# SSM groups of seven units with the gate inside, output halves under the last chunks, and a straight program

## The reference

```python
proj = u @ w_in
gl, cb, cc, cx, z, xbc, dt = jnp.split(proj, split_at, axis=-1)
...
xbc = jax.nn.silu(causal_depthwise_conv(xbc, ssm_conv_w) + ssm_conv_b.astype(xbc.dtype))
...
y = ssd_scan(xs * dt[..., None], dt * a, bs, cs)
y = y + d_skip.astype(jnp.float32)[:, None] * xs
y = y.reshape(bsz, seqlen, D_SSM) * jax.nn.silu(z.astype(jnp.float32))
yg = y.reshape(bsz, seqlen, SSM_GROUPS, D_SSM // SSM_GROUPS)
yg = yg * lax.rsqrt(jnp.mean(yg * yg, axis=-1, keepdims=True) + EPS)
y = (yg.reshape(bsz, seqlen, D_SSM) * ssm_norm_w.astype(jnp.float32)).astype(u.dtype)
p_ssm = y @ w_ssm_out
g_conv, g_ssm = jnp.split(jax.nn.sigmoid(gl), 2, axis=-1)
merged = g_conv * p_conv + g_ssm * p_ssm
```

## Time and profile before

| | us |
|---|---|
| median of 3 runs | 1856.3 |
| lowest and highest | 1855.08, 1859.28 |
| the profiled execution's own time | 1858.3 |
| its span in the trace | 1856.6 |
| TensorE busy | 1772.2 (95%) |
| VectorE, ScalarE, GpSimd busy | 1056.3, 794.6, 239.9 |

### The profile page before, as it was taken

How to read it: one execution, slowest core, us unless ns; L and a number is a source line. 1 busy time by engine, 2 the same in 40 slices (tenths; PEclk the granted TensorE clock), 3 DMA queues, 4 the chain that set the end, 5 groups by cost and what they waited for, 6 DMA issues and landing times.

```text
span 1856.6 us, 25724 instructions
## 1 busy us (share of the span) xinstructions
PE 1772.2 (95%) x8482; PEld 1456.2 (78%) x8482; DVE 1056.3 (57%) x1492; ACT 794.6 (43%) x1137; POOL 239.9 (13%) x312
## 2 busy tenths in 40 slices
PE   6889999999999999989999999999999989999997
PEld 4667777777888888868888888878897778888885
DVE  3677777775236666548855665685556343333333
ACT  4365666665222222355413443664433375224522
POOL 0101111110001220022111225211110200000001
PEclk8999999999999999989999999999999999999999
DMA  9143333332525664326655563111111323322331
GB/s 305 53 127 112 106 109 104 102 114 75 175 91 181 196 193 141 105 65 204 203 169 175 188 221 113 56 49 44 46 58 57 102 68 102 101 92 91 102 102 56
DMA packets 70501, 220.71 MB, mean 119 GB/s; under 512 B 8992, under 2 KB 17312, under 8 KB 70432
## 3 DMA queue, kind: packets, MB, share of 16 engines
q1 hardware_dynamic: 51664, 160.73, 26.8%
q0 software_dynamic: 17632, 56.83, 9.8%
q10 hardware_dynamic: 1136, 2.23, 0.4%
HBM read 217.52 MB, written 2.23 MB: 118 GB/s over the span
## 4 chain that ended last, share of the span: by engine, by line
PE 73%; DVE 10%; ACT 6%; DVEq 5%; issue 3%; ACTq 2%; DMA 1%; SPq 0%; POOL 0%
PE bank L385 19%; PE bank L386 19%; PE bank L387 19%; PE bank L1033 2%; PE bank L1034 2%; PE bank L1035 2%; DVE xs L717 1%; DVEq L738 1%; DVE bc L717 1%; PE bank L416 1%; DVE es L740 1%; PE bank L417 1%; PE bank L418 1%; PE bank L1086 1%; PE bank L1084 1%
## 5 line engine op out<-in xcount | busy, mean ns | idle before, releaser
L371 DVE TENSOR_TENSOR wlo<-wraw,whi 128x1024 fp32r<-128x1024 f32 x280 | 353.4, 1263 | 251.7 <-ACT whi L360 232.9
L360 ACT ACTIVATE whi<-wraw 128x1024 fp32r<-128x1024 f32 x280 | 295.8, 1058 | 441.2 <-PE bank L387 363.2
L385 PE MATMUL bank<-uhi,whi 128*128 128x512 f32 x1212 | 478.4, 395 | 2.1 <-DVE wlo L371 2.1
L386 PE MATMUL bank<-ulo,whi 128*128 128x512 f32 x1212 | 472.4, 390 | 0.0
L387 PE MATMUL bank<-uhi,wlo 128*128 128x512 f32 x1212 | 472.4, 390 | 0.0
L385 PE MATMUL bank<-vhi,whi 128*128 128x512 f32 x688 | 268.1, 390 | 0.0
L387 PE MATMUL bank<-vhi,wlo 128*128 128x512 f32 x688 | 267.7, 389 | 0.0
L386 PE MATMUL bank<-vlo,whi 128*128 128x512 f32 x688 | 267.6, 389 | 0.0
L385 PEld LDWEIGHTS bank<-uhi,whi 128*128 128x128 f32 x1212 | 228.1, 188 | 48.9 <-DVE wlo L371 2.6
L387 PEld LDWEIGHTS bank<-uhi,wlo 128*128 128x128 f32 x1212 | 228.0, 188 | 48.0
L386 PEld LDWEIGHTS bank<-ulo,whi 128*128 128x128 f32 x1212 | 228.3, 188 | 46.2 <-issue 0.2
(11 more groups left out here) (354 smaller groups left out, 2213.2 us busy)
## 6 DMA issues: line engine op xcount, KB each, us to landing
wraw<-in_units SPq DMA_DIRECT2D x280, 512.0 KB, 3.5
aring<-in_ada POOLq DMA_DIRECT2D x160, 256.0 KB, 3.7
slab<-in_ada SPq DMA_DIRECT2D x32, 256.0 KB, 6.9
es<-decay_rows POOLq DMA_DIRECT2D x32, 256.0 KB, 3.8
eac<-decay_rows POOLq DMA_DIRECT2D x32, 128.0 KB, 2.9
x<-in_xT SPq DMA_DIRECT2D x2, 1024.0 KB, 9.2
xr<-in_xT ACTq DMA_DIRECT2D x1, 2048.0 KB, 12.5
outT<-xr SPq DMA_DIRECT2D x8, 256.0 KB, 2.1
```

The lines of the kernel that those rows point to most:

```text
L360: act.activation(whi[:, at % SLOTS, :], wraw[:, at % RAW, :], ACT.Copy).then_inc(w_hi, 1)
L371: dve.tensor_tensor(wlo[:, at % SLOTS, :], wraw[:, at % RAW, :], whi[:, at % SLOTS, :].bitcast(f32), ALU.subtract).then_inc(w_split, 1)
L385: pe.matmul(out, wh, rhs_hi(k), start=first and k == 0, stop=False)
L386: pe.matmul(out, wh, rhs_lo(k), start=False, stop=False)
```

## The change

The order of the weight units and of the work around them is changed from the SSM groups to the output:

- Groups 1 to 7 have seven units: two of the six, one unit of the output's gate as unit 2, then the other four. ScalarE copies the gate's bank to `mg`. The taps stand in slots 0, 1, 3 and 4, the first z unit is unit 5, the second unit 6. ScalarE's silu of the first z unit and the squares are in slot 5; so is `pe_n`, behind a0; a1 is in slot 6. The silu of the second z unit comes ahead of the first convolution of the next group.
- `gate_ssm` is gone. A phase `tail` has the eighth unit of the gate, then the first halves of three outputs with b1 to b3 in between, then the second halves of these three in turn over the tiles, with `pe_n` after three tiles and waits for `f_fin` at each tile; then the fourth output's two halves. Four outputs are left for `ssm_out`.
- The sigmoids are eight activations on `mg`, one after the other, behind the last norm.
- Groups 1 to 7 and the output are straight code in place of loops; SyncE takes the units' order from a list.

```diff
 PHASES = [
     ("ssm0", 6, [0, 1, 2, 3, 0, 1], 1),
-    ("ssm", 12, [2, 3, 0, 1, 2, 3, 0, 1, 2, 3, 0, 1], 3),
-    ("ssm7", 6, [2, 3, 0, 1, 2, 3], 1),
-    ("gate_ssm", 8, [0, 1, 2, 3, 0, 1, 2, 3], 1),
-    ("ssm_out", 4, [0, 1], 4),
+] + [(f"ssm{g}", 7, [(7 * g - 1 + n) % 4 for n in range(7)], 1) for g in range(1, SSM_GROUPS)] + [
+    ("tail", 9, [3, 0, 1, 2, 3], 1),
+    ("ssm_out", 4, [0, 1], 2),
     ("conv", 4, [0, 1, 2, 3], 8),
     ("conv_out", 4, [0, 1, 2, 3], 2),
     ("w_o", 4, [0, 1, 2, 3], 2),
...
+
+
+def ssm_units():
+
+    gate, out = 6 * SSM_GROUPS, 6 * SSM_GROUPS + KT
+    order = list(range(6))
+    for g in range(1, SSM_GROUPS):
+        order += [6 * g, 6 * g + 1, gate + g - 1, 6 * g + 2, 6 * g + 3, 6 * g + 4, 6 * g + 5]
+    order += [gate + KT - 1] + [out + 2 * j for j in range(3)] + [out + 2 * j + 1 for j in range(3)]
+    return order + list(range(out + 6, out + 2 * KT))
...
-        def pe_slot(pe, k, g, par_, prev):
-
-            q = 1 - par_
-            if prev and k == 0:
-                pe_b(pe, g - 1, q, 0)
-                pe_a(pe, g - 1, q, 2)
-            if prev and k == 1:
-                pe_b(pe, g - 1, q, 1)
-                pe_a(pe, g - 1, q, 3)
-            if prev and k in (2, 3):
-                pe_b(pe, g - 1, q, k)
-            if prev and k == 5:
+        def pe_slot(pe, n, g, prev, here):
+            par_ = g % 2
+            if prev and n < 4:
+                pe_b(pe, g - 1, 1 - par_, n)
+                if n < 2:
+                    pe_a(pe, g - 1, 1 - par_, n + 2)
+            if here and n in (5, 6):
+                pe_a(pe, g, par_, n - 5)
+            if prev and n == 5:
                 pe_n(pe, g - 1)
-            if k in (4, 5) and not tail(g):
-                pe_a(pe, g, par_, k - 4)
-
-        def tail(g):
-            return isinstance(g, int) and g == SSM_GROUPS
...
-        def act_slot(act, k, g, par_, prev, it, ph, ku, here):
-
-            if 1 <= k <= 4 and here:
-                act_silu(act, g, par_, k - 1)
-            if here and k < 4:
-                act_conv(act, g, par_, k, it, ph, ku)
-            if prev and k == 0:
-                act.wait_ge(unit_done, 6 * g)
-                act_gate(act, 5, 1 if par_ else 3)
-            if here and k == 4:
-                wait_unit(act, ph, it, ku)
-                wait(act, S["f_y"], g)
-                act_gate(act, 4, PH[ph]["banks"][ku])
-            if k == 4 and prev:
+        def act_slot(act, n, g, prev, here):
+
+            par_, ph = g % 2, f"ssm{g}"
+            if prev and n == 0:
+                last = 7 * g - 2
+                act.wait_ge(unit_done, last + 1)
+                act_gate(act, 5, last % 4)
+            if here and n in (1, 2, 4, 5):
+                act_silu(act, g, par_, {1: 0, 2: 1, 4: 2, 5: 3}[n])
+            if here and n in (0, 1, 3, 4):
+                act_conv(act, g, par_, {0: 0, 1: 1, 3: 2, 4: 3}[n], 0, ph, n)
+            if here and n == 2:
+                wait_unit(act, ph, 0, n)
+                act.activation(mg[:, g - 1, :], bank(ph, n)[:], ACT.Copy)
+                act.drain().then_inc(freed(ph, n), 1)
+            if here and n == 5:
+                wait_unit(act, ph, 0, n)
+                act.wait_ge(S["f_y"], g)
+                act_gate(act, 4, PH[ph]["banks"][n])
+            if prev and n == 5:
                 act.wait_ge(S["f_y"], g)
                 act.activation(sqs[:], ys[:, 1 - par_, :, :], ACT.Square).then_inc(S["f_sq"], 1)
-            if k == 5:
+            if n == 6:
...
-        def dve_slot(dve, k, g, par_, prev, here):
-            if prev:
-                q = 1 - par_
-                if k == 0:
-                    dve_b(dve, g - 1, q, 0)
-                if k in (1, 2):
-                    dve_a(dve, g - 1, k + 1)
-                    dve_b(dve, g - 1, q, k)
-                if k == 4:
-                    dve_b(dve, g - 1, q, 3)
-                    dve.wait_ge(S["z_s"], 2 * g)
-                    dve.tensor_tensor(ys[:, q, :, :], ys[:, q, :, :], zs[:], ALU.mult).then_inc(S["f_y"], 1)
-            if here and k < 4:
-                dve_taps(dve, g, par_, k)
-            if k == 5:
...
+        def dve_slot(dve, n, g, prev, here):
+            par_ = g % 2
+            q = 1 - par_
+            if prev and n < 3:
+                if n > 0:
+                    dve_a(dve, g - 1, n + 1)
+                dve_b(dve, g - 1, q, n)
+            if prev and n == 4:
+                dve_b(dve, g - 1, q, 3)
+                dve.wait_ge(S["z_s"], 2 * g)
+                dve.tensor_tensor(ys[:, q, :, :], ys[:, q, :, :], zs[:], ALU.mult).then_inc(S["f_y"], 1)
+            if here and n in (0, 1, 3, 4):
+                dve_taps(dve, g, par_, {0: 0, 1: 1, 3: 2, 4: 3}[n])
+            if here and n == 5:
+                dve.wait_ge(S["cv_s"], 4 * g + 4)
+                for v in range(2):
+                    last = dve.tensor_scalar(ys[:, par_, v, :], xs[:, v, :], pcd("d_skip", 2 * g + v), None, ALU.mult)
+                last.then_inc(S["y_skip"], 1)
+                dve.drain()
+            if here and n == 6:
+                dve_a(dve, g, 0)
+                dve_a(dve, g, 1)
+            if prev and n == 6:
...
+            for g in range(1, SSM_GROUPS):
+                for n in range(7):
+                    split_hi(act, f"ssm{g}", 0, n)
+                    act_slot(act, n, g, True, True)
+            split_hi(act, "tail", 0, 0)
+            act_slot(act, 0, SSM_GROUPS, True, False)
+            split_hi(act, "tail", 0, 1)
+            wait_unit(act, "tail", 0, 0)
+            act.activation(mg[:, KT - 1, :], bank("tail", 0)[:], ACT.Copy)
+            act.drain().then_inc(freed("tail", 0), 1)
+            for n in range(2, 5):
+                split_hi(act, "tail", 0, n)
+            act_slot(act, 5, SSM_GROUPS, True, False)
+            act_slot(act, 6, SSM_GROUPS, True, False)
+            for j in range(KT):
+                act.activation(mg[:, j, :], mg[:, j, :], ACT.Sigmoid).then_inc(N2["gl_s"], 1)
+                if j == 3:
+                    split_hi(act, "tail", 0, 5)
             act.wait_ge(S["f_fin"], SSM_GROUPS)
             act.dma_start(xr[:], xT.rearrange("(k p) t -> p k t", p=P)).then_inc(N2["x2_ld"], 16)
+            for n in range(6, 9):
+                split_hi(act, "tail", 0, n)
...
+            dve_slot(dve, 5, 0, False, True)
+            dve_slot(dve, 6, 0, False, True)
+
+            for g in range(1, SSM_GROUPS):
+                for n in range(7):
+                    split_lo(dve, f"ssm{g}", 0, n)
+                    dve_slot(dve, n, g, True, True)
+            for n in range(3):
+                split_lo(dve, "tail", 0, n)
+                dve_slot(dve, n, SSM_GROUPS, True, False)
+            split_lo(dve, "tail", 0, 3)
+            dve_slot(dve, 4, SSM_GROUPS, True, False)
+            split_lo(dve, "tail", 0, 4)
+            dve_slot(dve, 6, SSM_GROUPS, True, False)
...
-            def ssm_out(it):
+            def gated_out(j, bank_, free):
+
+                dve.wait_ge(N2["gl_s"], j + 1)
+                dve.tensor_tensor(mg[:, j, :], mg[:, j, :], bank_[:], ALU.mult)
+                dve.drain().then_inc(free, 1)
+            split_lo(dve, "tail", 0, 5)
+            for j in range(3):
+                wait_unit(dve, "tail", 0, 4 + j)
+                gated_out(j, bank("tail", 1 + j), freed("tail", 1 + j))
+                split_lo(dve, "tail", 0, 6 + j)
+            wait_unit(dve, "tail", 0, 8)
+            gated_out(3, bank("tail", 4), freed("tail", 4))
...
+            for g in range(1, SSM_GROUPS):
+                for n in range(7):
+                    if (g, n) != (1, 0):
+                        pe_unit(pe, f"ssm{g}", 0, n, u_h, u_l)
+                    pe_slot(pe, n, g, True, True)
+
+            def half(h, at=0):
+                return (lambda t: v_h(t + at + 8 * h)), (lambda t: v_l(t + at + 8 * h))
+
+            pe_unit(pe, "tail", 0, 0, u_h, u_l)
+            pe_slot(pe, 0, SSM_GROUPS, True, False)
+            pe.wait_ge(S["f_fin"], SSM_GROUPS // 2)
+            for n in range(1, 4):
+                pe_unit(pe, "tail", 0, n, *half(0), out_i=n, last=False)
+                pe_slot(pe, n, SSM_GROUPS, True, False)
+            for n in range(4, 7):
+                pe.wait_ge(w_split, PH["tail"]["u0"] + n + 1)
+            for t in range(KT):
+                pe.wait_ge(S["f_fin"], SSM_GROUPS - 1 if t < 6 else SSM_GROUPS)
+                for n in range(4, 7):
+                    slot = (PH["tail"]["u0"] + n) % SLOTS
+                    wh, wl = whi[:, slot, t * P:(t + 1) * P], wlo[:, slot, t * P:(t + 1) * P]
+                    out = bank("tail", n - 3)[:]
+                    pe.matmul(out, wh, v_h(t + 8), start=False, stop=False)
+                    pe.matmul(out, wh, v_l(t + 8), start=False, stop=False)
+                    mm = pe.matmul(out, wl, v_h(t + 8), start=False, stop=t == KT - 1)
+                    if t == KT - 1:
```

(59 more changed lines are left out.)

55 lines of the change are left out of this document (2 added, 53 removed).

## The result

The changed kernel takes 1863.51 us in the median of 16 runs (1859.23 to 1866.3), against 1856.88 us of the kernel before on the same chips (16 runs, 1854.22 to 1859.28). The ratio is 1.0033, 95% interval 1.0025 to 1.0041: slower by 0.33%, some 6.6 us. The forecast was 1863.8 us.

A forecast was written before the change was run, and what follows sets the result against it. TensorE was taken to set the time, with gaps in its row to win. Removed waits -19.7, new wait +19.2 and clock +8 gave +7.5 us on the 1856.3 us median: 1863.8 us, own range 1860 to 1868, wider range 1855.5 to 1871.

The forecast's parts named there:

- The new wait at `pe_n`: Slot 5, groups 1 to 7: TensorE waits 2.75 us each for silu, squares and GpSimd's addition; 19.2 us added.
- The removed waits: SSM groups: TensorE's waits for VectorE's `dve_b` and ScalarE's last silu go; 19.7 us removed, other bound 15.
- the loop's register work goes too: Loop of the SSM groups: register work is not on TensorE's path; its removal was given nothing.
- a full cover: SSM groups: TensorE without gaps would give back 19.7 us, all taken as removed.
- VectorE's cycle: SSM groups: VectorE's and ScalarE's cycle grows from 45.3 to 48.4 us a group, against 50.0 that TensorE will need.
- VectorE staying behind: Rival: silu ahead of the first convolution delays VectorE's taps, b3 waits again; seven groups give 7 us more, 1871 us; chance 0.13.
- The clock, 8 us: Behind the new gaps at `pe_n`: clock falls in 5 or 6 of 7 groups, 1.5 us each; bounds 0 and 11.
- The rows that I argued from: Gaps of 2.06 us near 83 us and 1.72 near 1293: clock behind them 0.57 and 0.50 of full speed.
- The rule of the Trainium skill: Ground for the rival that the clock holds through the new gaps: 1856 to 1859 us, chance 0.15.
- The tail, 0 us: Tail: units 4 to 6 in turn over the tiles cover the last group's 6.3 us chain by 0.7 us; 0 added.
- "Same" or slower: Whole kernel against a 0.2% (3.7 us) threshold: slower by more 0.72, within 0.17, faster 0.11.

The follow-up runs named there:

- the filled gap: Changed kernel with eleven float32 128x128 matmuls on constants between a0 and `pe_n` in slot 5 of groups 1 to 7: 1853.71 us, ratio 0.9982.
- the last experiment: Kernel with `pe_n` one unit later, VectorE's lo part of slot 1 made three times (2.6 us more a group): 1845.75 us, ratio 0.9929.

## Why the prediction was right, and where it was not

The time, 1863.8 against 1863.51, is closer than its parts deserve. The sum was -19.7 + 19.2 + 8 = +7.5 us; the medians of the experiments make it -23.1 + 19.9 + 9.8 = +6.6. Each term was too small, and the errors on the two sides nearly cancel: that is luck.

1. **The new wait at `pe_n`, 7 x 2.75 = 19.2 us.** Right, in place, cause and size: seven waits of 2.65 us as idle time; by periods it is 50.04 - 47.11 = 2.93 us a group, and by the filled gap 19.9 us in all.

2. **The removed waits, 19.7 us.** Right in size: with the wait out of the way the changed part is 20.3 us shorter in the profiled executions (the medians are 23.1 us apart, and the rest lies outside the part, in code that is the same). The cause was half wrong. The step that failed is "the loop's register work goes too; it isn't on TensorE's path, and I give it nothing". Straight code alone gave 14.5 us, VectorE's alone 13.3. The seventh unit and the order around it have the rest when they come second: from the straight kernel of before, 1842.45, to `pe_n` one unit later, 1833.83, 8.6 us. I had read the sum of the gaps from TensorE's rows and could have seen the cause in the same trace, which has this `pe_n` of group 6 beside those of the earlier trace rows:

```profile
369.51 1.13 PE L620 MATMUL bank<-sqs,con 128*128 128x512 f32 x2
```

   Group 7, the straight one, takes 413.28 - 369.51 = 43.8 us, where the loop's groups take (369.51 - 143.71) / 5 = 45.2. The sum held since a full cover is the same whoever gives it; a forecast of nothing for straight code alone would have been wrong by 14.5 us. Seven units in a loop were never run, so how much of the waits the new order alone would have removed stays open.

3. **VectorE's cycle, 48.4 us a group.** Too high for the changed kernel, for the same reason: it was put together from the loop's 45.3 us. Without the wait TensorE runs at 47.11 us and waits for nothing. An estimate of VectorE's own cycle comes from the last experiment: its period of 48.67 less the 2.6 us added is 46.1 us. With the 2.2 us a group that the loop cost before it would be 48.3, near my 48.4. By this estimate seven units in a loop would still have fitted into the changed kernel's 50.0 us, and it is the faster version, 47.11 us a group, that needs the straight code. The rival that rested on this number, VectorE staying behind, had no ground in straight code, though the mechanism is real once the margin is gone.

4. **The clock, 8 us.** That falls would follow the new gap in most groups is right, and five or six at 1.5 us were near the mark: four in the profiled execution, and 9.8 us over the runs' medians, about six by estimate. The rows that I argued from were weaker than I took them to be. The clock had fallen behind idle times of 1.72 and 2.06 us, but with 1.76 us in each group it never did. What stands beside the gap differs, small products in the old places and full units here, and I didn't try that. But the same gap doesn't always end the same way either. The one near 85 us lies ahead of the part that was changed and stands in all 13 profiled executions, with 2.05 to 2.07 us. Behind it the clock fell in 11 of them and not in two, the kernel before as straight code and the last experiment; in the first of these two, TensorE's row and the busy table with the clock:

```profile
85.42 0.43 PE L2289 MATMUL bank<-con,dd 32*128 32x32 f32 x4 [2.07 <-DVE dac L2078]
...
86.00:90.00 4.00, 3.56 (x17) 2.85 (x16) 3.85 (x6) 3.27 (x7) 1.57 (x2) 1.00 0.54 164
```

   The gap of 1.72 us came back with ScalarE alone straight, near 1290 us, and the clock held. So one gap with a fall behind it says little about the next of its length, and that two such rows gave nearly the right number is partly luck. What decides it stays open. The rule of the Trainium skill ("TensorE: Matmul & The Clock Gate", "Why this matters for your kernels": keep gaps between bursts of matmuls under about 3 us) would have put the result at 1856 to 1859 us. These traces don't agree with it as a safe bound: 2.65 us made the clock fall in four and five of seven groups in two profiles, 2.2 us in four of seven, and 2.06 us near 85 us in 11 of 13 profiles.

5. **The tail, 0 us.** Right. In the changed kernel `pe_n` starts at 495.22 and the chain to `f_fin` ends at 501.5, 6.3 us later as forecast, and no wait shows; without the turn over the tiles, in the kernel of `pe_n` one unit later, it costs 9.6 us.

6. **"Same" or slower.** I gave 0.72 to slower by over 0.2%; it is 0.33%. The profiled execution alone would have said 0.2% (3.9 us of span), as its part behind the change happened to be 2.8 us shorter.

The changed kernel is, then, 29.7 us away from a version that differs in where one matmul instruction stands.

## What to carry to other kernels

When work is moved to a later slot, move what consumes it by as much: count, for each wait, how many units stand between its producer and its consumer before and after. An engine that is only 74% busy can still be the pace of a cycle, and then tenths of a microsecond between its instructions count (here 2.2 of some 3 us a group); take a straight copy of the loop as the first test. A short wait on TensorE that comes back in each group costs more than its length when the clock falls behind it; filling it with products that nobody needs is a cheap way to measure that part. Look at the same gap in several profiles before taking one fall, or none, for a rule.

## What I had not expected of the hardware

- The loop on VectorE, with run-time offsets and the register instructions for them, cost 13.3 us in six groups of 45 us, 2.2 a group, in a kernel where VectorE is 74% busy.
- 77 matmuls more made the program 9.8 us faster than leaving TensorE idle in the same places.
- The step between idle times of TensorE that leave the clock alone and such as lower it is narrow here, and not sharp: 1.76 us in seven groups, no fall; 2.2 us, four of seven in the profiled execution; 2.65 us, four and five of seven in two profiles and about six by the medians.
- One and the same idle time of 2.06 us, ahead of the changed part, was followed by a fall in 11 of 13 profiled executions and by none in the other two.
